# Hyena stage in a new order, transforms copied out by ScalarE, filter network inside the input projection

## The reference

```python
def hyena_kernels_f(L, pw1, pb1, pw2, pb2, pw3, freq):
    ...
    hid = jnp.sin(fr * (z @ pw1.astype(f32) + pb1.astype(f32)))
    hid = jnp.sin(fr * (hid @ pw2.astype(f32) + pb2.astype(f32)))
    h = (hid @ pw3.astype(f32)).reshape(L, 2, HY_ORDER, HY_WIDTH)
    ...
    h = h * jnp.exp(-t[:, None] * deltas[None, :])[:, None, None, :]
    k_two = jnp.concatenate([h[:, 0], jnp.zeros((1, HY_ORDER, HY_WIDTH), f32), h[:0:-1, 1]], axis=0)
    k_two = k_two / jnp.sum(jnp.abs(k_two), axis=0, keepdims=True)
    return jnp.fft.rfft(k_two, axis=0)

def hyena(u, sw, sb, pw1, pb1, pw2, pb2, pw3, freq, skip):
    u = centred_conv3(u, sw, sb)
    v, x1, x2 = jnp.split(u, 3, axis=-1)
    kf = hyena_kernels_f(L, pw1, pb1, pw2, pb2, pw3, freq)
    z = v
    for o, gate in enumerate((x1, x2)):
        zf = jnp.fft.rfft(z.astype(jnp.float32), n=2 * L, axis=1)
        conv = jnp.fft.irfft(zf * kf[None, :, o], n=2 * L, axis=1)[:, :L]
        z = gate * (conv.astype(z.dtype) + skip[o] * z)
    return z
```

## Time and profile before

| what | us |
|---|---|
| median of 3 runs | 2764.09 (2754.27 to 2770.19) |
| the profiled execution's own time | 2764.57 |
| its span in the profile | 2762.7 |
| input projection, first to last PE matmul | about 46 to 316 |
| attention | about 317 to 433 |
| last convolution and Hyena on DVE | 434.4 to 631.2 |
| output projection begins on PE | 631.6 |

### The profile page before, as it was taken

The page is one execution under the profiler, slowest core; times in us unless marked ns, Lnnn a source line. Parts: engine busy times, 40 slices in busy tenths (PEclk is TensorE's granted clock), DMA queues, the critical chain, the costliest instruction groups (busy, mean ns, idle before and its releaser), DMA issues. The chain is left out here.

```text
span 2762.7 us, 53378 instructions
## 1 busy us (share of the span) xinstructions
PE 2353.0 (85%) x23840; PEld 1948.7 (71%) x23840; DVE 1024.6 (37%) x1468; ACT 630.4 (23%) x939; POOL 835.2 (30%) x699
## 2 busy tenths in 40 slices
PE   6899977689699999999489957888888847899997
PEld 3678744446499999999169946777776735688786
DVE  3000276771400000122774035777777631200123
ACT  4100364211410000122312123333333211211111
POOL 2132100000134433443034412222222213366662
PEclk8999998899799999999589978999999968899999
DMA  5555500001011112121113411111111111122232
GB/s 229 209 198 219 195 17 15 1 31 38 23 61 61 61 61 66 57 63 52 17 61 113 128 65 39 38 39 39 39 39 37 22 62 61 61 91 96 90 96 69
DMA packets 139277, 204.25 MB, mean 74 GB/s; under 512 B 87783, under 2 KB 97511, under 8 KB 131912
## 3 DMA queue, kind: packets, MB, share of 16 engines
q1 hardware_dynamic: 139080, 201.26, 22.8%
HBM read 183.93 MB, written 17.30 MB: 73 GB/s over the span
## 5 line engine op out<-in xcount | busy, mean ns | idle before, releaser
L258 POOL CAST TMP_r<-WR 128x1024 fp32r<-128x1024 f32 x120 | 126.2, 1052 | 809.9 <-DMA WR<-in_ffn_w_dram 480.5
L277 PE MATMUL PS<-H_r,TMP_r 128*128 128x384 f32 (+1 forms) x1104 | 336.4, 360 | 17.8 <-DVE Y_r L484 13.7
L277 PE MATMUL PS<-Y_r,TMP_r 128*128 128x384 f32 (+1 forms) x1104 | 336.3, 360 | 9.2 <-POOL WR_r L260 5.4
L260 POOL TENSOR_TENSOR WR_r<-WR,TMP_r 128x1024 fp32r<-128x1024 f32 x120 | 288.9, 2407 | 9.6
L407 DVE TENSOR_TENSOR P<-TMP,PS 128x768 f32 (+1 forms) x44 | 36.1, 821 | 577.7 <-PE PS L277 577.7
L277 PEld LDWEIGHTS PS<-H_r,TMP_r 128*128 128x128 f32 x1104 | 206.5, 191 | 35.1 <-DVE Y_r L484 14.8
L277 PEld LDWEIGHTS PS<-Y_r,TMP_r 128*128 128x128 f32 x1104 | 205.7, 191 | 25.3 <-POOL WR_r L260 5.9
L277 PE MATMUL PS<-H_r,WR_r 128*128 128x384 f32 x752 | 196.2, 342 | 0.0
L268 POOL CAST TMP_r<-WR 128x1024 fp32r<-128x1024 f32 x68 | 85.7, 1261 | 335.2 <-DMA WR<-in_rw_w_rkv_dram 180.3
L270 POOL TENSOR_TENSOR WR_r<-WR,TMP_r 128x1024 fp32r<-128x1024 f32 x68 | 166.7, 2451 | 5.4
L580 PE MATMUL PS<-H_r,TMP_r 128*128 128x384 f32 x704 | 152.0, 338 | 3.2 <-DVE H_r L618 2.2
(11 more groups left out here) (290 smaller groups left out, 4476.5 us busy)
## 6 DMA issues: line engine op xcount, KB each, us to landing
WR<-in_ffn_w_dram SPq DMA_DIRECT2D x88, 512.0 KB, 3.4
TMP<-in_mod_w_dram SPq DMA_DIRECT2D x40, 1024.0 KB, 4.9
WR<-in_down_dram SPq DMA_DIRECT2D x44, 512.0 KB, 3.6
WR<-in_mix_w_in_dram SPq DMA_DIRECT2D x24, 512.0 KB, 5.9
WR<-in_rw_w_rkv_dram SPq DMA_DIRECT2D x24, 512.0 KB, 4.2
P<-in_mod_w_dram SPq DMA_DIRECT2D x4, 2048.0 KB, 22.0
vkr_dram<-extra SPq DMA_DIRECT2D x16, 384.0 KB, 4.8
scan_front<-vkr_dram SPq DMA_DIRECT2D x16, 384.0 KB, 3.1
```

Source lines behind the costliest of these rows:

```text
L258: nc.gpsimd.tensor_copy(hi, raw).then_inc(weights_hi, 1)
L260: nc.gpsimd.tensor_tensor(lo, raw, hi.bitcast(F32), ALU.subtract).then_inc(weights_split, 1)
L277: last = nc.tensor.matmul(PS[:, bank + b, 0:h1 - h0], w, x[:, h0:h1], start=k + p == 0, stop=k == CT - 1 and p == 2)
```

## The change

1. The filter network leaves the Hyena stage. Its eight small loads (`network_sp`) stand before the first weight tiles in SP's queue. Its four half-width matmuls stand on PE behind the tiles 1, 3, 7 and 12 of the input projection (`network_pe`), the sines on ACT two tiles later (`network_act`), the arguments on DVE between the modulation columns (`network_dve`).
2. Both pairs of banks of a transform are copied out by ACT (two instructions in place of one). DVE forms the sum from two SBUF tiles and the difference as (odd x -2) + sum, in one fused instruction.
3. The pieces of all four runs have a new order on PE, ACT and DVE, with new banks; the waits follow. The last two convolutions (j = 1, 2) stand inside the Hyena order on DVE, so that the first filters and transposes begin after j = 0.

```diff
@@ network, in the input projection
+        NETWORK_AT = (1, 3, 7, 12)
...
+                if t in NETWORK_AT:
+                    network_pe(pe, *divmod(NETWORK_AT.index(t), 2))
...
+                if t - 2 in NETWORK_AT:
+                    network_act(act, *divmod(NETWORK_AT.index(t - 2), 2))
...
+        def network_pe(pe, k, h):
+            i = 2 * k + h
+            w, x, rows = ((PW1[0:EMB, :], FEATS[0:EMB, :], HID), (PW2[0:HID, :], HIDP[0:HID, :], 128))[k]
+            pe.wait_ge(net_in, 16 * 8)
+            pe.wait_ge(mod_added, (1, 1, 2, 3)[i])
+            if i:
+                pe.wait_ge(dve_step, 6 * (i - 1) + 1)
+            if k:
+                pe.wait_ge(mlp_hid, h + 1)
+            nc.tensor.matmul(PS[0:rows, MOD_TURN, 0:HALF], w, x[:, HALF * h:HALF * h + HALF], start=True, stop=True)\
+              .then_inc(mlp_mm, 1)
@@ order of the engines' streams
             inputs_sp(sp)
+            network_sp(sp)
             inproj_sp(sp)
...
+            for i in range(2):
+                network_dve(v, chain, 0, i)
             for g in range(1, NMOD):
                 mod_cols_dve(v, g)
+                if g < 3:
+                    network_dve(v, chain, 1, g - 1)
@@ transforms
             def even(r, f, bank, name, dst):
                 act.wait_ge(HPE.sem, HPE[f"{name}d{r}.{f}"])
-                HAC.done(nc.scalar.activation(dst[r % 2][:, f, :, 1, :], PS[:, bank:bank + 2, 0:HW], ACT.Copy),
+                nc.scalar.activation(dst[r % 2][:, f, :, 0, :], PS[:, bank:bank + 2, 0:HW], ACT.Copy)
+                HAC.done(nc.scalar.activation(dst[r % 2][:, f, :, 1, :], PS[:, bank + 2:bank + 4, 0:HW], ACT.Copy),
                          f"{name}e{r}.{f}")
...
-                HDV.done(nc.vector.tensor_tensor(plus, minus, odd, ALU.add), f"{name}p{r}.{f}")
+                HDV.done(nc.vector.tensor_tensor(plus, plus, minus, ALU.add), f"{name}p{r}.{f}")
                 v.wait_ge(HDV.sem, HDV[f"{name}p{r}.{f}"])
-                HDV.done(nc.vector.tensor_tensor(minus, minus, odd, ALU.subtract), f"{name}b{r}.{f}")
+                HDV.done(nc.vector.scalar_tensor_tensor(minus, minus, -2.0, plus, ALU.mult, ALU.add), f"{name}b{r}.{f}")
@@ the order of PE, its first and last pieces
-            mlp(0, 0)
             pe.wait_ge(attn_out, STEPS)
-            pe.wait_ge(conv3_done, 12)
...
+            pe.wait_ge(conv3_done, 10)
+            filters(0, 1, 0)
+            filters(0, 0, 2)
...
+            inverse(3, 0, 0)
+            sums(3, 2)
@@ SP
-            sp.wait_ge(HPE.sem, HPE["sum3"])
+            sp.wait_ge(HPE.sem, latest(HPE, ("sum2", "sum3", "kd2.1")))
```

More of the change, by code:

```diff
@@ L972, in hybrid_dit_kernel @@
[L972 to L979, removed]
-            kp2.1 kb2.1 fm3.0 fm3.1 mx3.0 mx3.1 {product_marks("2.1")} kp3.0 kb3.0 zp3.0 zb3.0 rec2 rn2 rec3 rn3 {product_marks("3.0")}
-            st2.0 z2.0 st2.1 z2.1 st2.2 z2.2 st2.3 z2.3 st3.0 z3.0 st3.1 z3.1 st3.2 z3.2 st3.3 z3.3""")
@@ L982, in hybrid_dit_kernel, with latest @@
-        HPO = Ledger("hy_pool", """neg drop add0.1 add0.2 add0.3 add1.1
-            add2.1 add2.2 add2.3 add3.1""")
+        def latest(ledger, names):
+            return max(ledger[at] for at in names)
+        HPE = Ledger("hy_pe", """fl0.1 fl0.0 fl0.3 fl0.2 zt0.1 zt0.2 zt0.0 zt0.3 fl1.1 zd0.0 kd0.0 kd0.1 fl2.1 fl1.0 zd0.1 sum0 fl2.3
+            kd1.0 zt1.1 zt1.0 fl2.0 fl2.2 iv0.0 iv0.1 iv0.2 iv0.3 zd1.0 kd2.0 zt2.1 zt2.3 zt2.2 zt2.0 fl3.1 fl3.0
+            zd2.0 iv1.0 iv1.1 iv1.2 iv1.3 zd2.1 sum1 sum2 kd2.1 zt3.1 zt3.0 kd3.0 zd3.0 iv2.0 iv2.1 iv2.2 iv2.3
+            iv3.0 iv3.1 iv3.2 iv3.3 sum3""")
@@ L1007, in hyena_sp @@
             sp.dma_start(TURN_BACK, a["dft512"][:, 2048:4096]).then_inc(turn_in, 16)
-            sp.wait_ge(HPE.sem, HPE["sum3"])
+            sp.wait_ge(HPE.sem, latest(HPE, ("sum2", "sum3", "kd2.1")))
         def hyena_pe(pe):
[L1013 to L1017, removed]
-                for h in range(2):
-                    last = nc.tensor.matmul(PS[0:rows, bank + h, 0:HALF], w, x[:, HALF * h:HALF * h + HALF],
-                                            start=True, stop=True)
-                HPE.done(last, f"mlp{k}")
             def turn(r, k, bank):
@@ new lines, in hyena_pe @@
+            inverse(0, 0, 0)
+            pe.wait_ge(HAC.sem, HAC["ke1.0"])
+            turn(1, 1, 4)
+            turn(1, 0, 5)
+            filters(2, 0, 6)
+            pe.wait_ge(HAC.sem, HAC["zt1.0"])
+            filters(2, 2, 4)
+            inverse(0, 1, 0)
+            pe.wait_ge(HDV.sem, HDV["fm2.2"])
+            waves(1, 0, 4)
+            pe.wait_ge(HAC.sem, HAC["sc0.3"])
+            kernels(2, 0, 0)
+            pe.wait_ge(HAC.sem, HAC["ze1.0"])
+            turn(2, 1, 4)
+            turn(2, 3, 5)
@@ new lines, in hyena_pe @@
+            turn(2, 2, 6)
+            turn(2, 0, 7)
+            pe.wait_ge(HAC.sem, HAC["ke2.0"])
+            filters(3, 1, 0)
+            filters(3, 0, 2)
+            pe.wait_ge(HAC.sem, HAC["zt2.3"])
+            waves(2, 0, 4)
+            pe.wait_ge(HDV.sem, HDV["fm3.0"])
+            inverse(1, 0, 2)
+            pe.wait_ge(HAC.sem, HAC["ze2.0"])
+            waves(2, 1, 4)
+            pe.wait_ge(HDV.sem, HDV["fm3.1"])
+            sums(1, 0)
+            sums(2, 1)
+            pe.wait_ge(HAC.sem, HAC["ze2.1"])
```

446 lines of the change are left out of this document (230 added, 216 removed).

## The result

The changed kernel took 2728.07 us, the median of four runs (2727.5 to 2730.8), beside 2763.85 us for the kernel before on the same chip (2754.27 to 2770.19). The ratio is 0.9875, 95% interval 0.9846 to 0.9905: 35.8 us less, well beyond the 13.8 us that the prediction takes for what a measurement can tell from no change. The prediction was 2727, from a sum of 2727.4. The profiled execution took 2727.5 us, its span is 2725.7.

The account below looks back on a forecast made before the run. PE bounds the input projection; in Hyena neither PE nor DVE is the bound, they wait for each other in turn. 2764.57 - 39.8 + 2.1 + 0.5 = 2727.4 us, predicted 2727, range 2713 to 2744.

Parts of the forecast that it names:

- walk of the stage: Followed the new order on all engines through Hyena with durations from rows: 157.0 us against 196.8; bounds -46 to -30.
- leg A: From the Hyena stage's start to VectorE's first filter transform, set by TensorE: 30.9 us.
- leg B: VectorE's work in Hyena from the first filter transform on, TensorE then nearly always ahead: 117.0 us.
- its waits, with that for sum3: VectorE's waits in leg B: 4.6 us, plus 1.6 for sum3 after TensorE restarts at the low clock.
- meetings with GpSimd: GpSimd's adds in Hyena slowing VectorE instructions beside them: three meetings, 0.95 us more each, 2.9 in all.
- seam: Hyena's end to the output projection: taken as 0; 1.5 us if the first weights took 6.3 to land.
- ScalarE empties the transforms alone: Twelve more copies of 1.02 us in Hyena: a cost between 0 and 12.2 us, 3 of it in the legs.
- new order: Reordered pieces in Hyena, walked with the network already out: stage 157.0 against 196.8 us, -39.8.
- Rival 1: In Hyena VectorE waits for ScalarE's copies: +12.2 us if all 12 are exposed, 2739.6; chance 0.11, wholly or in part.
- Rival 2: In Hyena the order gives nothing, only the network's removal does: about 11 us, total 2756; chance 0.05.
- Network in the projection: Four matmuls in the input projection, 0.66 us each, one of them free: +2.1 us with handing over.
- Small loads: Eight loads ahead of the first weights in SP's queue: +0.5 us, between 0 and 2.

Follow-up runs that it names:

- e10: The changed kernel itself once more, unaltered, on the chip of e9: 2726.12 us, ratio 0.9864.
- e3: The changed kernel with the old emptying: ScalarE copies one pair, VectorE reads the other from PSUM, TensorE waits for the difference; two swaps on VectorE: 2769.56 us, ratio 1.0017.
- e5: The changed kernel, ScalarE still copying all banks, but TensorE waits for VectorE's difference before reusing them; two swaps on VectorE: 2770.66 us, ratio 1.0021.
- e6: Control: the changed kernel with only the two swaps on VectorE that e3 and e5 needed: 2727.82 us in a single run.
- e1: The kernel before with only the filter network moved into the input projection; old order, banks and copies: 2765.83 us, ratio 1.0006.
- e7: The changed kernel with each of the four network matmuls in the projection issued five times into the same bank: 2737.87 us, ratio 0.9894.
- e4: The changed kernel with the eight small loads issued behind the first four weight tiles instead of ahead: 2733.07 us in a single run.
- e9: The changed kernel with both edits, that of e8 and that of e4: 2728.83 us, ratio 0.9859.
- e2: The kernel before with only the copies changed: ScalarE copies all four banks, TensorE waits for the copies; old order, network in the stage: 2768.1 us, ratio 1.0008.
- e11: The changed kernel with fourteen stand-in VectorE instructions for the network's two chains, TensorE waiting for the last ahead of the first filters: 2741.7 us, ratio 0.992.
- e8: The changed kernel with TensorE's convolution wait moved down to the transposes and VectorE's first filter ahead of the second convolution: 2724.4 us in a single run.

## Why the prediction was right, and where it wasn't

The span fell by 37.0 us, predicted were 37.2. The stage gave 3.7 us more than predicted, the parts ahead of it took 5.4 more, and the part behind, whose spread is 14 us, happened to be 1.7 shorter: the walk of the stage earned its number within 4 us, the rest of the agreement is luck. By the prediction's steps, from the profiled execution:

| step | predicted | after |
|---|---|---|
| leg A | 30.9 | 30.5 (e10 31.5) |
| leg B, VectorE's work | 117.0 | 117.3 |
| its waits, with that for sum3 | 4.6 + 1.6 | 2.4 (e10 3.8) |
| meetings with GpSimd | 2.9 | 3.0, in four places |
| stage | 157.0, -39.8 | 153.3, -43.5 |
| before the stage | +2.6 | +8.0 |
| seam | 0 | +0.2 |
| behind | 0 | -1.7 |

**The walk of the stage** held in its terms. VectorE's first sum of a filter's transform starts 30.5 us into the stage:

```profile
472.94 1.23 DVE L1373 TENSOR_TENSOR Y<-Y 128x1024 f32<-128x1024 f32 x1 [3.78 <-ACT Y L1223]
474.19 1.22 DVE L1375 SCALAR_TENSOR_TENSOR Y<-Y 128x1024 f32<-128x1024 f32 x1
```

The fused difference, priced 0.1 dearer for each, takes what the plain one took, 1.22 us; that term of 1.1 was wrong. (117.3 is what is left of leg B without waits and meetings; what in it makes up for the 1.1 was not traced.) Products take 9.6 us (494.99 to 504.59), as before. The wait for kd2.1's copies, 1.7 in the sum, was 0.28 in after and 2.00 in e10: there the prediction took the slower of two cases. TensorE's restart ahead of sum3 was there, but VectorE waited 0.40 us for it, not 1.6. Of the two waits of TensorE that the walk had, the one of 6.0 us ahead of inverse(3,0) came, with 5.5 us; the one of 3.9 ahead of inverse(0,1) did not. TensorE, the same 32 records without and with idle time ahead:

```profile
535.13 3.73 PE L1114 MATMUL PS<-TMP,P 128*128 128x128 f32 x32
...
583.94 5.75 PE L1114 MATMUL PS<-TMP,P 128*128 128x128 f32 x32 [5.48 <-DVE P L1346]
```

VectorE at the inversion of sum3:

```profile
590.52 0.18 DVE L1405 RECIPROCAL hyc<-PS 128x4 f32<-128x4 f32 x1 [0.40 <-PE PS L1101]
```

**Meetings with GpSimd.** The prediction had three, 2.9 us in all. The trace has four, 3.0 us: three of 0.95 us and a partial one of 0.2. One of them is the one that the prediction named. GpSimd's add beside zp1.0 and zb1.0:

```profile
519.80 2.18 POOL L1355 TENSOR_TENSOR WR<-WR,TMP 128x512 f32<-128x512 f32 x1 [5.40 <-DVE TMP L1399]
```

VectorE's sum and difference there:

```profile
519.64 1.22 DVE L1373 TENSOR_TENSOR P<-P 128x1024 f32<-128x1024 f32 x1
520.89 2.18 DVE L1375 SCALAR_TENSOR_TENSOR P<-P 128x1024 f32<-128x1024 f32 x1
```

The sum was under way when the add came, and kept its 1.22; the difference behind it took 2.18. The Trainium skill (SBUF — State Buffer, "SBUF: two separate sides") says of a VectorE instruction with two SBUF inputs and a GpSimd instruction that reads SBUF that whichever starts first has the port pair for its whole length and that the other is blocked. These rows agree, and show that the loser is not always the one that was expected: the prediction named the sum.

**The step that failed: "ScalarE empties the transforms alone".** It was priced by itself, as a cost between 0 and 12.2 us, of which 3 in the legs. The release of the banks stood in it as a remark with no number. By e3 and e5 against after and e6 (192.1 and 196.8 against 153.3 and 155.9) that remark is the gain: between 36 and 43.5 us in this order. The number of the stage was right because the walk had the banks released by ScalarE built in; its -39.8 stood under "new order", where e3 shows the stage at -4.7 and e5 at 0.0 with the same order and the network gone as well. The bound "0 where all is hidden" was wrong: the part had to be allowed to give time as well as cost it. The same walk with the old waits would have shown the sign and most of the size; in e3's expectation it gave 26 of the 38.8 us.

**The rival that fell.** Rival 1 had VectorE waiting for ScalarE's copies. (These waits were VectorE's largest in sum before, 22.5 us, but not the longest, as the prediction has it: one at L1366, released by TensorE, took 5.9 us against 5.5.) It waits for them 5.9 us in the stage, 5.6 of these in leg A, where TensorE's transforms come last, and 0.28 behind it. The Trainium skill (TensorEngine Tiling (Array Packing), "PSUM Bottleneck") advises to empty PSUM with both engines; here e3 does just that and takes 2769.56 us, and the kernel with one engine 2728.07; with one engine and the late release, in e5, it is 2770.66. What decides here is not how many engines read the banks but whose queue the last reading stands in.

**Rival 2**, the order gives nothing and only the network's removal does, is half right for this kernel without the early release: in e3 and e5 the order gives nothing, and the network's removal gives nothing either (2769.56 and 2770.66 us, where the rival had 2756). Its price was wrong: 11 us for two chains of VectorE, 3.8 in e1.

**Network in the projection.** By e7 the matmuls cost 2.2 to 2.8 us, predicted 2.1. No TensorE wait stands at them. The one behind tile 1 takes 1.54 us, not 0.66, but TensorE's waits for modulation chunks there fell from 7.0 to 5.4 us in sum, so that it is free, as predicted. TensorE's timeline at the first:

```profile
80.96 1.94 PE L1518 MATMUL PS<-TMP,CS 128*32 128x512 f32 x8 [3.92 <-DMA TMP<-in_mod_w_dram]
82.82 1.54 PE L1025 MATMUL PS<-P,hyc 33*64 33x384 f32 x2
```

**Small loads.** Predicted +0.5, between 0 and 2; 1.6 at the start. The prediction took 4.5 us of issue for all eight from three loads at a quiet time; ahead of the weights they hold the queue for 13.9 us. That it was blocked anyway was right in kind (12.3 of these are given back before the first cast), and 1.6 is what is left.

**What was not in the sum.** Of the 8.0 us before the stage, 2.2 to 2.8 and 1.6 are these. Attention starts 5.4 us later in the mean of the ten kernels with the network unchanged in the projection (322.9) than in the two without (317.1 and 317.9); attention itself is the same code and takes between 117.2 and 121.3 us. Some 1 to 1.6 us of the projection and the spread of attention have no cause that was shown. e4 and e9 say that an earlier start doesn't take them back.

**Seam.** As predicted, TensorE is released by VectorE:

```profile
596.28 4.18 PE L335 MATMUL PS<-Hraw,WR 128*128 128x384 f32 x6 [5.80 <-DVE Hraw L1417]
```

It starts 0.58 us behind the last gate in place of 0.36.

## What to carry to other kernels

In this kernel a PSUM bank is free when the last engine that reads it comes to that instruction in its queue. Before you let an engine run behind, look whether it holds such a last reading, and move it to one with a shorter queue, even if that costs copies (here 12 of 1.02 us). The move by itself may give nothing, as in e2. Price the parts of a change together and apart: here neither of the two that were tried alone shows a gain, order and removal without the early release show none either, and the three together are worth 36 us. A walk that holds them all gives the right total and can still give the wrong reason.

## What the runs showed of the hardware

- In this stage waits of TensorE cost more than themselves. In e3 24 us more idle time came with 14.8 us more busy time for the same 480 records, at a granted clock of 0.86 against 0.96. Single records: 9.20 us behind 7.76 us of idle time, 7.03 with none.
- The same code can get another clock at the same place. The transform behind 0.41 us of idle time took 7.13 us in after, e4, e6 and e11, and 8.83 in e7, e8, e9 and e10; the granted clock was 1.00 in after and 0.81 in e10.
- A fused instruction of VectorE on two SBUF operands of 1024 elements took 1.22 us, as the plain sum did, and 2.18 us beside an add of GpSimd.
- Eight small loads ahead of 2 MB of weights in SP's queue held it for 13.9 us and cost the weights 1.6 us.
